# RWKV-7 recurrence on one core: chunk systems inverted as two 16x16 diagonal blocks with the corner on TensorE; key path and masks on GpSimd, gram copies on ScalarE

## The chip, the cores and the metric

One core of a Trainium2 chip runs the whole program. The metric is the device time of one execution in microseconds; the comparison is made on medians of several executions.

## What is computed

The program is a chain of layers (attention, a retrieval feed-forward layer, two more mixers with their feed-forward layers). The change touches only the last mixer, an RWKV-7 time mixing over 256 tokens, 16 heads of 64:

```python
def rwkv7_step(state, inp):
    r_t, w_t, k_t, v_t, a_t, b_t = inp
    sa = jnp.einsum('bhvk,bhk->bhv', state, a_t)
    state = (state * w_t[:, :, None, :] + sa[..., None] * b_t[:, :, None, :]
             + v_t[..., None] * k_t[:, :, None, :])
    return state, jnp.einsum('bhvk,bhk->bhv', state, r_t)
...
    a = jax.nn.sigmoid((a0 + (xa @ a1) @ a2).astype(f32))
...
    kk = heads(k * k_k.astype(f32))
    kk = kk / jnp.maximum(jnp.sqrt(jnp.sum(kk * kk, axis=-1, keepdims=True)), 1e-12)
    k = k * (1.0 + (a - 1.0) * k_a.astype(f32))
...
    seqs = (tm(r_h), tm(w_h), tm(k_h), tm(v_h), tm(-kk), tm(kk * a_h))
    _, y = lax.scan(rwkv7_step, jnp.zeros((B, H, N, N), f32), seqs)
```

The kernel does not scan token by token. It works in chunks of 32 tokens (`C`), 8 chunks (`CT`) in 2 tiles (`NT`) of 128 tokens. Within a chunk the tokens depend on each other through a strictly triangular 32x32 matrix for each head, so a unit triangular system has to be inverted for each of the 32 pairs of tile and head (`NS`) in each of the 4 chunks of a tile; across chunks a 64x64 state for each head is carried.

## The kernel before, in words

`project_mixes` (L2958) makes the projections R, K, V in twelve weight blocks: ScalarE casts a block (`make_high`), VectorE makes its low half (`make_low`, L3080), TensorE multiplies, ScalarE empties the bank (L3064). In its last two blocks VectorE also makes `raw` = K times the row k_k, its sums and its normalisation (L3124 to L3133). GpSimd does nothing in it. Each such function is one `nc.Block`; the engines meet at its end, and the next function starts when the last of them has finished.

`wkv` (L3145) is the recurrence. Each engine has a queue of its own written out by hand, and the queues meet in semaphores. In order of time:

1. Low-rank products on TensorE, their biases added by VectorE (L3571) in the order L tile 0, A tile 0, L tile 1, A tile 1; sigmoids on ScalarE (L3476); sums of the decays on TensorE (L3281); exponentials on ScalarE (L3469, L3487) into `up`, `down`, `before`.
2. VectorE makes the scaled operands: `key_factor` (L3582), `rate_key` (L3588), `scale_r` (L3592), `scale_keys` (L3598, L3600) for each tile, later `key` (L3585) and `tt(Kd, K, down)` (L3611, L3616). Each is one pass over 128x1024 floats.
3. TensorE turns each scaled operand (`flip`, L3304), in eight jobs: r, a, kk of tile 0, the same of tile 1, then k of both. ScalarE and VectorE place the turned halves (`place`, L3218 to L3223), and `grams` (L3312) multiplies them: 128 small matmuls for each of four calls.
4. VectorE masks the grams out of PSUM (`mask`, L3558): those of a into `GA`, those of k into `GK`.
5. VectorE inverts all the systems at once: it transposes 32x32 blocks (L3620), runs 31 steps of a product (L3625) and a sum (L3627), and transposes back (L3636). The masks of `GK` (after steps 4 and 10) and the products `K * rest` (after step 14, L3634) stand inside this loop.
6. Meanwhile TensorE makes the remaining decays (L3335), the decays at the chunk ends (L3340), the products within a chunk (L3349, which need `GK`), and the key-value products (L3358). ScalarE empties them (L3511, L3515).
7. With the inverses and all of `KV` in place, TensorE applies the inverses (`w2` L3366, `w1` L3375), and seven steps carry the state from chunk to chunk (`write` L3387, read L3423, `grow` L3647). Normalisation and gate follow; `mix_out_to_end` (L3753) is the next block.

GpSimd clears two tiles at the start (L3746, L3748) and one later (L3750). SyncE loads three rows at the start of `wkv`. `slot(i)` is a buffer of the weight ring, 128x2048 floats; slots 4 and 5 hold the inversion.

Of the kernel before, what the change touches and what calls it, by code (L numbers as in the profile page):

```python
# [19 lines left out]
ALU = mybir.AluOpType  # L20
# [122 lines left out]
class Kit:  # L143
# [17 lines left out]
    def dve(self, ins):  # L161

        self.nc.vector.wait_ge(self.step["dve"].sem, self.step["dve"].up(ins))

# [2793 lines left out]
def project_mixes(kit, dram, R, K, V, A, KK, L, G, rs):  # L2958
# [19 lines left out]
    kk_row, biases = place(6)[:, 0:D], place(9)  # L2978
# [3 lines left out]
    with kit.sb("mix_high", [P, 2, KD, SEQ], F32R) as x_hi, kit.sb("mix_low", [P, 2, KD, SEQ], F32R) as x_lo, \  # L2982
# [7 lines left out]
        def _(sp):  # L2990
# [6 lines left out]
            kk_in.up(sp.dma_start(kk_row, bcast(dram["rw_kk_2"], D)), 16)  # L2997
            sp.wait_ge(split.sem, p0 + 10)
# [78 lines left out]
        def _(dve):  # L3077
# [26 lines left out]
            for b in range(1, nb):  # L3104
# [15 lines left out]
                if b == nb - 2:  # L3120
                    dve.wait_ge(kk_in.sem, 16)
# [23 lines left out]
def wkv(kit, dram, R, K, V, A, KK, L, G, wide_in, rows, chunks, Kd, turned1, twa, tgb, st, bonus, PC):  # L3145
# [29 lines left out]
    XT, terms = (slot(4)[:, i * C * C:(i + 1) * C * C].rearrange("p (j t) -> p j t", j=C) for i in range(2))  # L3175
    sy = slot(5)[:, 0:C * C].rearrange("p (j t) -> p j t", j=C)
    inv = slot(5)[:, C * C:2 * C * C].rearrange("p (u t) -> p u t", t=C)
# [12 lines left out]
    grams_a, grams_k, masked_a, masked_k = (kit.count(n) for n in ("grams_a", "grams_k", "masked_a", "masked_k"))  # L3190
    cleared, solved = kit.count("inverse_cleared"), kit.count("solved")
# [7 lines left out]
    with kit.sb("arT", [P, NT, 2 * KD, 5, C]) as arT, \  # L3199
            kit.sb("gram_a", [P, NS, 2 * C]) as GA, kit.sb("state", [P, KD, HD]) as S, \  # L3200
            kit.sb("state_part", [P, KD, HD]) as part, nc.Block() as block:
        GK = wide_in[:].rearrange("p t n -> p (t n)").rearrange("p (u j) -> p u j", j=2 * C)
# [37 lines left out]
        def _(sp):  # L3240
            for i, row in enumerate((dram["rw_ka_2"], dram["rw_rk_2"].rearrange("e h d -> e (h d)"))):
                rows_in.up(sp.dma_start(rows[:, i], bcast(row, D)), 16)
            rows_in.up(sp.dma_start(chunks[:], dram["chunks"]), 16)

            for T in range(NT):
                sp.wait_ge(within_out.sem, 4 * (T + 1))
                sp.wait_ge(masked_k.sem, 2 * NT)
# [16 lines left out]
        def _(pe):  # L3264
# [42 lines left out]
            def grams(T, keys, j, bank, columns_of, done):  # L3307
                for half in range(2):
                    wait_placed(pe, j, half)
                for hh in range(RH):  # L3310
# [3 lines left out]
                    if hh // 2 == KD - 1:  # L3314
                        done.up(mm)
# [3 lines left out]
            grams(0, BT, 2, 0, first_a, grams_a)  # L3319
# [3 lines left out]
            grams(1, BT, 5, 2, first_a, grams_a)  # L3323
            flip(6)
            grams(0, KT, 6, 6, block_of, grams_k)
            flip(7)
            pe.wait_ge(masked_a.sem, 2)
            grams(1, KT, 7, 0, block_of, grams_k)
# [79 lines left out]
            for n, T, c in steps[1:]:  # L3408
# [27 lines left out]
                if n in (CH, CH + 1):  # L3436
                    share(0, n - CH, range(CH))
# [549 lines left out]
```

## Time and profile before

| what | before |
|---|---|
| three runs | 2704.85, 2705.49, 2709.05 us; median 2705.49 |
| span of the profiled execution | 2706.4 us |
| busy in the span | TensorE 2380.3, VectorE 1862.4, ScalarE 1218.7, GpSimd 622.8 us |
| `wkv` in the span | 2349.55 to about 2485.5 us |
| GpSimd in `wkv` | three memsets |

The span is what the profiler recorded of one execution, from the first to the last instruction. Starts are microseconds from the start of the span. A row of the timeline has the start, the time taken, the engine, the line, the operation, what is written and read, the shapes, the number of instructions merged, and in brackets how long the engine was idle before it and what ended that ("issue" is a wait for nothing that the profile shows). PE is TensorE, DVE VectorE, ACT ScalarE, POOL GpSimd. Two further facts of the page are used below: queue 8 moved the instructions, 85 packets and 1.39 MB, some 16 KB each; TensorE had 12882 matmuls, each with a weight load.

### The profile page before, as it was taken

To read this page: it belongs to the slowest core of one execution; us is meant where nothing else is said; L and a number is where in the kernel's file an instruction comes from. 1 tells how busy PE (TensorE), PEld (TensorE's weight loads), DVE (VectorE), ACT (ScalarE), POOL (GpSimd) and SP (SyncE) were. 2 spreads that over 40 slices of the span, in tenths; PEclk is the share of its full clock that TensorE was granted. 3 is DMA by queue.
4 is the path that set the end of the run, shared out by engine and by line. 5 is a ranking of instruction groups with operands and counts; after the bars stand their busy time and mean duration, and the time that the engine had idled before them with its cause. 6 is when DMAs were issued, how large, how long until landed. Compare 5 with 4: busy or idle time off the path is not lost. (4 is left out here: it accounts for less than half of the span.)

```text
span 2706.4 us, 35151 instructions
## 1 busy us (share of the span) xinstructions
PE 2380.3 (88%) x12882; PEld 1586.5 (59%) x12882; DVE 1862.4 (69%) x3462; ACT 1218.7 (45%) x2588; POOL 622.8 (23%) x529
## 2 busy tenths in 40 slices
PE   6988788888888988888778799999999998977999
PEld 4774334333334444343333268898888887866887
DVE  4767866677667867867765666676667666797665
ACT  3433434444444544444434454457445444534543
POOL 0003444554444434455544400000000000000000
PEclk9988999999999999999999999999999998977999
DMA  9789999999999999999999945542555554212553
GB/s 386 257 329 423 403 427 427 424 427 424 424 411 418 376 426 411 427 427 427 427 424 426 427 160 186 186 156 98 183 186 181 188 188 165 91 50 111 179 187 116
DMA packets 121706, 811.27 MB, mean 300 GB/s; under 512 B 15713, under 2 KB 18825, under 8 KB 26584
## 3 DMA queue, kind: packets, MB, share of 16 engines
q0 software_dynamic: 74160, 540.05, 47.7%
q1 hardware_dynamic: 47400, 269.32, 27.5%
q8 instruction: 85, 1.39, 0.2%
q14 instruction: 61, 0.50, 0.0%
HBM read 807.12 MB, written 1.15 MB: 299 GB/s over the span
## 5 line engine op out<-in xcount | busy, mean ns | idle before, releaser
L1402 PE MATMUL bank<-rows,diag 128*128 128x512 f32 (+1 forms) x2060 | 995.9, 620 | 212.6 <-ACT diag L1559 212.1
L1797 DVE CUSTOM_DVE_ANT_0 rows<-rows,h 128x1024 f32<-128x1024 f32 (+1 forms) x512 | 620.3, 1224 | 359.7 <-DMA rows<-in_peer_rows,idx 353.3
L1402 PEld LDWEIGHTS bank<-rows,diag 128*128 128x128 f32 (+1 forms) x2060 | 371.8, 194 | 739.7 <-ACT diag L1559 421.1
L1281 POOL DMA_INDIRECT rows<-in_peer_rows,idx x512 | 609.0, 1189 | 741.5 <-PE bank L1402 679.3
L1550 ACT ACTIVATE picks<-picks 128x1 f32<-128x1 f32 (+1 forms) x512 | 103.3, 202 | 637.9 <-DVE picks L1797 617.5
L2142 PE MATMUL bank<-hT_pair,halves 128*128 128x512 f32 x864 | 307.2, 399 | 0.4 <-DVE hT_pair L2020 0.4
L2143 PE MATMUL bank<-hT_pair,halves 128*128 128x256 f32 x864 | 242.2, 280 | 0.0
L1559 ACT ACTIVATE diag<-const_table,picks 128x128 f32<-128x128 f32 (+1 forms) x512 | 205.5, 401 | 48.0 <-ACT picks L1554 1.1
L2076 DVE TENSOR_TENSOR halves<-weight_ring,halves 128x2048 fp32r<-128x2048 f32 x74 | 169.3, 2289 | 74.3 <-ACT halves L2071 74.1
L2142 PEld LDWEIGHTS bank<-hT_pair,halves 128*128 128x128 f32 x864 | 162.3, 188 | 40.9 <-DVE hT_pair L2020 0.9
L1314 PE MATMUL bank<-halves_b,halves_a 128*128 128x256 f32 x912 | 172.0, 331 | 0.0
L2071 ACT CAST halves<-weight_ring 128x2048 fp32r<-128x2048 f32 x74 | 141.3, 1911 | 50.3 <-PE bank L2151 27.0
L2143 PEld LDWEIGHTS bank<-hT_pair,halves 128*128 128x128 f32 x864 | 163.1, 189 | 0.8
L1554 ACT ACTIVATE picks<-picks 128x1 f32<-128x1 f32 (+1 forms) x512 | 150.8, 294 | 18.9 <-ACT picks L1550 0.4
L1314 PEld LDWEIGHTS bank<-halves_b,halves_a 128*128 128x128 f32 x912 | 125.0, 191 | 55.7 <-issue 55.7
L2076 DVE TENSOR_TENSOR halves_b<-weight_ring,halves_b 128x2048 fp32r<-128x2048 f32 x36 | 82.5, 2292 | 63.7 <-ACT halves_b L2071 63.7
L2142 PE MATMUL bank<-hT_pair,halves_b 128*128 128x512 f32 x336 | 119.4, 398 | 1.5 <-DVE work L2252 1.5
L3746 POOL MEMSET weight_ring<- 128x1024 f32 x1 | 1.0, 952 | 499.7 <-POOLq L2985 499.7
L2151 PE MATMUL bank<-halves_a,hidden 128*128 128x512 f32 x320 | 103.7, 395 | 0.0
L2076 DVE TENSOR_TENSOR halves_a<-weight_ring,halves_a 128x2048 fp32r<-128x2048 f32 x36 | 82.4, 2289 | 25.1 <-ACT halves_a L2071 25.1
L2071 ACT CAST halves_a<-weight_ring 128x2048 fp32r<-128x2048 f32 x36 | 69.0, 1916 | 59.4 <-PE bank L2151 57.4
L2143 PE MATMUL bank<-hT_pair,halves_b 128*128 128x256 f32 x336 | 94.2, 280 | 0.0
(571 smaller groups left out, 3772.2 us busy)
## 6 DMA issues: line engine op xcount, KB each, us to landing
weight_ring<-in_ffn_w_gate SPq DMA_DIRECT2D x44, 1024.0 KB, 4.7
weight_ring<-in_ffn_w_up SPq DMA_DIRECT2D x44, 1024.0 KB, 4.8
weight_ring<-in_ffn_w_down SPq DMA_DIRECT2D x44, 1024.0 KB, 4.8
mod_ring<-in_mod_w SPq DMA_DIRECT2D x16, 1024.0 KB, 7.5
weight_ring<-in_peer_w_q SPq DMA_DIRECT2D x16, 1024.0 KB, 11.3
half_ring<-in_mod_w SPq DMA_DIRECT2D x24, 512.0 KB, 7.2
rows<-in_mod_w SPq DMA_DIRECT2D x12, 1024.0 KB, 8.1
weight_ring<-in_attn_w_in SPq DMA_DIRECT2D x12, 1024.0 KB, 4.7
```

The lines of the kernel that those rows point to most:

```text
L1281: nc.gpsimd.indirect_dma_start(ring[:, s], None, dram["peer_rows"], bass.IndirectOffsetOnAxis(ap=idx[:, T, n:n + 1], axis=0)).then_inc(row ...
L1314: mm = nc.tensor.matmul(kit.bank[hh % 2][:, half * SEQ:(half + 1) * SEQ], w[:, k, half * P:(half + 1) * P], t[:, :, k, :], start=(k == 0 a ...
L1402: mm = nc.tensor.matmul(bank[:, :], diag[0:n, j % DIAG_SLOTS], ring[0:n, j % ROW_SLOTS, D + half * 512:D + (half + 1) * 512], start=(j in ...
L1550: gelued.up(nc.scalar.activation(its_dot, its_dot, ACT.Gelu_apprx_tanh))
L1554: scaled.up(nc.scalar.activation(its_weight, its_dot, ACT.Copy, scale=its_gate))
L1559: weighed.up(nc.scalar.activation(diag[r, j % DIAG_SLOTS], eye[r], ACT.Copy, scale=its_weight))
L1797: dotted.up(nc.vector.tensor_tensor_reduce(out=ring[r, s, 0:D], in0=ring[r, s, 0:D], in1=its_h, scale=1.0, scalar=0.0, op0=ALU.mult, op1=A ...
L2071: self.kit.nc.scalar.copy(hi, w).then_inc(self.high_made.sem, 1)
L2076: self.kit.nc.vector.tensor_tensor(lo, w, hi.bitcast(F32), ALU.subtract).then_inc(self.split.sem, 1)
L2142: nc.tensor.matmul(bank[:, :], w_hi[:, k, cols], halves.pair[:, k, :], start=(k == 0), stop=False, skip_group_check=True)
L2143: mm = nc.tensor.matmul(bank[:, SEQ:2 * SEQ], w_lo[:, k, cols], halves.hi[:, k, :], start=False, stop=(k == KD - 1), skip_group_check=True)
L2151: mm = self.kit.nc.tensor.matmul(self.kit.bank[4 + 2 * T + half][:, :], hidden[:, f % 2, s, T * P:(T + 1) * P], w[:, s, half * 512:(half + ...
```

## The change

What it does:

- The inverse of a 32x32 unit triangular system is built of its two 16x16 diagonal blocks (15 steps over both at once, instead of 31 steps) and a corner block, which is a product of three matrices. Two groups of 128 small matmuls on TensorE make the corner, one group ahead of the chunk-end decays and one behind them; four matmuls with the identity bring the lower diagonal block into the bank to which the corner is added. ScalarE copies between them.
- The key path moves from VectorE to GpSimd: four passes in `project_mixes` (K times k_a, subtracted from K), six in `wkv` (products with a, sums, products with `down`).
- The grams are copied out of PSUM by ScalarE; GpSimd masks them in SBUF, the one of k before the products within a chunk, the second half of the one of a before the shares of tile 0.
- The biases are added in the order L tile 0, L tile 1, A tile 0, A tile 1. The row k_a is loaded in `project_mixes`.

```diff
@@ project_mixes
             kk_in.up(sp.dma_start(kk_row, bcast(dram["rw_kk_2"], D)), 16)
+            kk_in.up(sp.dma_start(ka_row, bcast(dram["rw_ka_2"], D)), 16)
...
+        @block.gpsimd
+        def _(pool):
+            pool.wait_ge(made.sem, NT)
+            for T in range(NT):
+                kit.pool(nc.gpsimd.tensor_tensor(rated_part[:, T], K[:, T], ka_row, ALU.mult))
+                kit.pool(nc.gpsimd.tensor_tensor(K[:, T], K[:, T], rated_part[:, T], ALU.subtract))
@@ wkv, TensorE
-            pe.wait_ge(masked_a.sem, 2)
-            grams(1, KT, 7, 0, block_of, grams_k)
-
-            pe.wait_ge(masked_a.sem, 4)
+            pe.wait_ge(grams_out.sem, 2)
+            grams(1, KT, 7, 0, block_of)
+
+            pe.wait_ge(grams_out.sem, 4)
             for q in range(4):
...
+            pe.wait_ge(grams_out.sem, 6)
+            pe.wait_ge(solved.sem, 1)
+            for u in range(NS):
+                for c in range(CH):
+                    mm = nc.tensor.matmul(kit.bank[6][chunk(c), u * HC:(u + 1) * HC], GA[chunk(c), u, 0:C], own_blocks[chunk(c), u, 0:HC],
+                                          start=True, stop=True, tile_position=(c * C, c * C))
+            corner.up(mm)
+            for c in range(CH):
+                nc.tensor.matmul(kit.bank[7][chunk(c), :], kit.ident[chunk(c), chunk(c)], own_blocks[chunk(c), :, HC:],
+                                 start=True, stop=True, tile_position=(c * C, c * C))
             pe.wait_ge(exped.sem, 11)
...
             summed.up(mm)
+            pe.wait_ge(placed.sem, len(on_act) + 1)
+            for u in range(NS):
+                for c in range(CH):
+                    mm = nc.tensor.matmul(kit.bank[7][c * C:c * C + HC, u * HC:(u + 1) * HC], corner_t[chunk(c), u, :],
+                                          own_blocks[chunk(c), u, HC:], start=False, stop=True, tile_position=(c * C, c * C),
+                                          skip_group_check=True)
+            corner.up(mm)
             pe.wait_ge(exped.sem, 15)
 
             for T in range(NT):
-                pe.wait_ge(masked_k.sem, 2 * T + 2)
+                pe.wait_ge(masked.sem, T + 1)
+                if T:
+                    pe.wait_ge(placed.sem, len(on_act) + 2)
...
+                if n == CH:
+                    pe.wait_ge(masked.sem, NT + 1)
@@ wkv, ScalarE
-            place_next(len(on_act) - 4)
+            place_next(5)
+            copy_grams(GA, 0, 0)
+            copy_grams(GA, 1, 2)
+            place_next(2)
+            copy_grams(GK, 0, 6)
+            place_next(2)
+            copy_grams(GK, 1, 0)
             for T in range(NT):
                 exps(rest, T, 2 + 2 * T, -1.0, 5 + 2 * T)
+            act.wait_ge(corner.sem, 1)
+            placed.up(nc.scalar.copy(corner_t, kit.bank[6][:, :].rearrange("p (u t) -> p u t", t=HC)))
             act.wait_ge(summed.sem, 9)
...
+            act.wait_ge(corner.sem, 2)
+            placed.up(nc.scalar.copy(inv[:, :, HC:], kit.bank[7][:, :].rearrange("p (u t) -> p u t", t=HC)))
@@ wkv, VectorE
             def rate_key(T):
+                dve.wait_ge(key_rated.sem, T + 1)
                 step(tt(A[:, T], A[:, T], KN[:, T], mul))
...
-            key_factor(0)
             rate_key(0)
...
-            key(0)
             place_half(3)
-            k_scaled.up(tt(Kd[:, 0], K[:, 0], down[:, 0], mul))
-            mask(GA, P + 2 * C, grams_a, masked_a, 0, 0)
-            key(1)
             place_half(4)
             place_half(5)
-            k_scaled.up(tt(Kd[:, 1], K[:, 1], down[:, 1], mul))
-            mask(GA, P + 2 * C, grams_a, masked_a, 1, 2)
-
-            dve.wait_ge(masked_a.sem, 2 * NT)
+
+            dve.wait_ge(k_scaled.sem, NT)
+            dve.wait_ge(grams_out.sem, 2 * NT)
             step(nc.vector.transpose(sy.rearrange("p j t -> p t j"), GA[:, :, 0:C].rearrange("p u t -> p t u")))
...
-            for i in range(C - 1):
-
-                n, later = C - 1 - i, XT[:, 0:i + 1, i + 1:]
...
+            for i in range(HC - 1):
+                n, later = HC - 1 - i, x_blocks[:, :, 0:i + 1, i + 1:]
+                final = x_blocks[:, :, 0:i + 1, i].unsqueeze(3).to_broadcast([P, 2, i + 1, n])
+                shares = s_blocks[:, :, i, i + 1:].unsqueeze(2).to_broadcast([P, 2, i + 1, n])
+                step(tt(terms[:, :, 0:i + 1, 0:n], final, shares, mul))
+                step(tt(later, later, terms[:, :, 0:i + 1, 0:n], add))
+
+            nc.vector.transpose(own_blocks[:, :, 0:HC].rearrange("p u t -> p t u"), XT[:, 0:HC, :])
+            solved.up(nc.vector.transpose(own_blocks[:, :, HC:].rearrange("p u t -> p t u"), XT[:, :, HC:].rearrange("p j t -> p t j")))
+            solved.up(nc.vector.transpose(inv[:, :, 0:HC].rearrange("p u t -> p t u"), XT[:, :, 0:HC].rearrange("p j t -> p t j")))
+            for T in range(NT):
+                dve.wait_ge(exped.sem, 12 + 2 * T)
+                k_state.up(tt(K[:, T], K[:, T], rest[:, T], mul))
+            dve.wait_ge(solved.sem, 2)
@@ wkv, GpSimd
+            gtt = nc.gpsimd.tensor_tensor
+            for T in range(NT):
+                pool.wait_ge(rated.sem, NT + T + 1)
+                key_rated.up(gtt(rated_part[:, T], rated_part[:, T], A[:, T], ALU.mult))
+            for T in range(NT):
+                pool.wait_ge(key_rated.sem, T + 1)
+                kit.pool(gtt(K[:, T], K[:, T], rated_part[:, T], ALU.add))
+                pool.wait_ge(exped.sem, 5 * T + 4)
+                k_scaled.up(gtt(Kd[:, T], K[:, T], down[:, T], ALU.mult))
...
+            pool.wait_ge(rows_in.sem, 32)
+            for T in range(NT):
+                pool.wait_ge(grams_out.sem, 2 * NT + 2 * T + 2)
+                masked.up(mask(GK[:, T * RH:(T + 1) * RH, :], P, 2 * C))
+            masked.up(mask(GA[:, :, C:], P + 3 * C, C))
             pool.wait_ge(within_out.sem, 4 * NT)
```

## Rows read from the trace of the kernel before

**Rows 1.** Chain that ended last, 2349 to 2490 us: start, us, what.

```profile
2485.51 0.07 issue
...
2485.64 1.91 ACT halves L2071
```

**Rows 2.** Timeline, VectorE in `wkv`: start, us, engine, line, operation.

```profile
2363.01 1.22 DVE L3582 SCALAR_TENSOR_TENSOR key_decayed<-A,key_rows 128x1024 f32<-128x1024 f32 x1
...
2386.53 2.13 DVE L3620 STREAM_TRANSPOSE weight_ring<-gram_a 128x1024 f32<-128x1024 f32 x1
2388.69 0.19 DVE L3625 TENSOR_TENSOR weight_ring<-weight_ring 128x31 f32<-128x31 f32 x1
...
2391.18 0.30 DVE L3627 TENSOR_TENSOR weight_ring<-weight_ring 128x135 f32<-128x135 f32 x1
...
2416.76 2.07 DVE L3636 STREAM_TRANSPOSE weight_ring<-weight_ring 128x1024 f32<-128x1024 f32 x1
...
2423.48 2.36 DVE L3655 TENSOR_TENSOR weight_ring<-weight_ring,key_rows 128x1024 f32<-128x1024 f32 x2
2425.87 0.69 DVE L3642 COPY weight_ring<-bank 128x512 f32<-128x512 f32 x1
...
2428.39 0.82 DVE L3647 TENSOR_TENSOR state<-weight_ring,bank 128x256 f32<-128x256 f32 x2
```

**Rows 3.** Timeline, TensorE in `wkv`.

```profile
2373.96 1.48 PE L3312 MATMUL bank<-arT,hT 64*32 64x64 f32 x128
...
2383.21 2.04 PE L3312 MATMUL bank<-arT,turned_keys 64*32 64x64 f32 x128 [0.88 <-DVE arT L3221]
...
2394.27 3.70 PE L3335 MATMUL bank<-L,chunk_table 128*128 128x512 f32 x8
2397.81 3.63 PE L3340 MATMUL bank<-const_table,L 128*128 128x4 f32 x32
2401.75 5.61 PE L3349 MATMUL bank<-V,KK 32*64 32x64 f32 x250 [0.31 <-ACT chunk_decay L3506]
...
2411.47 1.80 PE L3358 MATMUL bank<-V,K 32*64 32x64 f32 x127 [2.97 <-issue]
2415.32 0.80 PE L3358 MATMUL bank<-V,K 32*64 32x64 f32 x34 [2.05 <-issue]
2418.97 0.28 PE L3366 MATMUL bank<-weight_ring 32*32 32x64 f32 x1 [2.86 <-DVE weight_ring L3636]
...
2426.33 0.73 PE L3375 MATMUL bank<-weight_ring,removal 32*64 32x32 f32 x33 [0.96 <-issue]
```

**Rows 4.** Timeline, ScalarE in `wkv`.

```profile
2391.89 0.59 ACT L3223 COPY turned_keys<-bank 128x512 f32<-128x512 f32 x1 [0.27 <-PE bank L3304]
...
2416.16 2.05 ACT L3515 COPY weight_ring<-bank 128x512 f32<-128x512 f32 x4 [2.02 <-PE bank L3358]
```

**Rows 5.** Groups of GpSimd by line: count, busy us, mean ns of one, idle before.

```profile
L2585 POOL TENSOR_TENSOR weight_ring<-weight_ring,const_table 128x384 f32<-128x384 f32 x4 | 4.0, 1007 | 294.1 <-DVE weight_ring L2640 294.1
```

**Rows 6.** Timeline, GpSimd beside VectorE in the retrieval layer.

```profile
1229.85 1.22 DVE L1797 CUSTOM_DVE_ANT_0 rows<-rows,h 128x1024 f32<-128x1024 f32 x1
1229.98 1.91 POOL L1281 DMA_INDIRECT rows<-in_peer_rows,idx  x1 [3.06 <-PE bank L1402]
...
1234.45 0.94 POOL L1281 DMA_INDIRECT rows<-in_peer_rows,idx  x1 [0.55 <-PE bank L1402]
...
1234.54 0.41 DVE L1950 MATCH_REPLACE8 hT<-ranks,hT 128x256 f32<-128x256 f32 x1
```

**Rows 7.** Timeline, the end of `project_mixes`, VectorE and ScalarE.

```profile
2339.17 2.29 DVE L3080 TENSOR_TENSOR low<-weight_ring,high 128x2048 fp32r<-128x2048 f32 x1 [1.20 <-ACT high L3037]
...
2344.62 2.36 DVE L3133 TENSOR_TENSOR weight_ring<-weight_ring,key_norms 128x1024 f32<-128x1024 f32 x2
...
2348.70 0.59 ACT L3064 COPY V<-bank 128x512 f32<-128x512 f32 x1 [4.50 <-PE bank L3023]
```

**Rows 8.** Busy time in a stretch: length, engines, granted clock, DMA share.

```profile
2380.00:2390.00 10.00, 6.74 (x269) 5.76 (x270) 7.90 (x13) 1.17 (x2) 0.00 (x0) 0.60 0.01 3
```

More of the change, by code:

```diff
@@ L163, in dve, with pool @@
         self.nc.vector.wait_ge(self.step["dve"].sem, self.step["dve"].up(ins))
+    def pool(self, ins):
+        self.nc.gpsimd.wait_ge(self.step["pool"].sem, self.step["pool"].up(ins))
     def act(self, ins):
@@ L3174, in wkv @@
     KV = W.ring[:, SLOTS // 2 + 1:SLOTS // 2 + 3, :].rearrange("p s (c n) -> p (s c) n", c=4)
[L3175 removed]
+    HC = C // 2
+    XT = slot(4)[:, 0:C * C].rearrange("p (j t) -> p j t", j=C)
+    terms = slot(4)[:, C * C:C * C + C * HC].rearrange("p (b j t) -> p b j t", b=2, t=HC)
     sy = slot(5)[:, 0:C * C].rearrange("p (j t) -> p j t", j=C)
+    on_diagonal = lambda i: slot(i)[:, 0:C * C + C].rearrange("p (b n) -> p b n", b=2)[:, :, 0:HC * C].rearrange("p b (j t) -> p b j t", t=C)[:, :, :, 0:HC]
+    own_blocks = slot(5)[:, 0:C * C].rearrange("p (u t) -> p u t", t=C)
     inv = slot(5)[:, C * C:2 * C * C].rearrange("p (u t) -> p u t", t=C)
@@ L3189, in wkv @@
     turned, placed, placed_dve = kit.count("wkv_turned"), kit.count("wkv_placed"), kit.count("wkv_placed_dve")
-    grams_a, grams_k, masked_a, masked_k = (kit.count(n) for n in ("grams_a", "grams_k", "masked_a", "masked_k"))
-    cleared, solved = kit.count("inverse_cleared"), kit.count("solved")
+    grams_made, grams_out, masked, key_rated = (kit.count(n) for n in ("grams_made", "grams_copied", "grams_masked", "key_rated"))
+    rated_part = by_tile(slot(5))
+    cleared, solved = kit.count("inverse_cleared"), kit.count("diagonal_solved")
+    corner = kit.count("corner_product")
     parted = kit.count("state_decayed")
@@ L3240, in _ @@
         def _(sp):
-            for i, row in enumerate((dram["rw_ka_2"], dram["rw_rk_2"].rearrange("e h d -> e (h d)"))):
-                rows_in.up(sp.dma_start(rows[:, i], bcast(row, D)), 16)
+            rows_in.up(sp.dma_start(rows[:, 1], bcast(dram["rw_rk_2"].rearrange("e h d -> e (h d)"), D)), 16)
             rows_in.up(sp.dma_start(chunks[:], dram["chunks"]), 16)
@@ L3305, in flip, with grams @@
                     turned.up(mm)
-            def grams(T, keys, j, bank, columns_of, done):
+            def grams(T, keys, j, bank, columns_of):
                 for half in range(2):
@@ L3554, in _ @@
             tt, stt = nc.vector.tensor_tensor, nc.vector.scalar_tensor_tensor
-            def mask(G, at, grams, masked, T, b):
-                for i in range(2):
-                    dve.wait_ge(grams.sem, 2 * T + i + 1)
-                    masked.up(tt(G[:, T * RH + i:(T + 1) * RH:2, :], kit.bank[b + i][:, :].rearrange("p (a t) -> p a t", t=2 * C),
-                                 chunks[:, at:at + 2 * C].unsqueeze(1).to_broadcast([P, KD, 2 * C]), mul))
             def place_half(j):
@@ L3565, in _ @@
             dve.wait_ge(bias_in.sem, 32)
-            for T in range(NT):
-                for m, dst in enumerate((L, A)):
+            for m, dst in enumerate((L, A)):
+                for T in range(NT):
                     for i in range(2):
@@ L3577, in _ @@
                     biased.up(tt(quarter(before, 2 * T + i), kit.bank[4 + 2 * T + i][:, :], quarter(L, 2 * T + i), ALU.subtract))
-            dve.wait_ge(rows_in.sem, 48)
-            def key_factor(T):
-                dve.wait_ge(rated.sem, NT + T + 1)
-                step(stt(out=Kd[:, T], in0=A[:, T], scalar=-1.0, in1=rows[:, 0], op0=add, op1=mul))
-            def key(T):
-                step(stt(out=K[:, T], in0=Kd[:, T], scalar=1.0, in1=K[:, T], op0=add, op1=mul))
+            dve.wait_ge(rows_in.sem, 32)
             def rate_key(T):
+                dve.wait_ge(key_rated.sem, T + 1)
                 step(tt(A[:, T], A[:, T], KN[:, T], mul))
```

40 lines of the change are left out of this document (19 added, 21 removed).

## The prediction

> **What bounds the kernel now.** I read the chain of work that ended last first. It is of no use inside the recurrence: it enters at 2485.6 us, where the next block starts [rows 1]. The engines meet at the end of each block, so what counts is when the last of them leaves `wkv`, and that has to be read from the timelines. VectorE first [rows 2]: from the key factor at 2363.01 it is hardly idle until it has transposed the inverses back, 2416.76 + 2.07 = 2418.83. Its 62 instructions of inversion run from 2388.69 to 2416.76, 0.19 us each at the start and 0.30 us with 135 elements. Then TensorE [rows 3]: the first inverse is applied at 2418.97, and the bracket names VectorE. The reader is tempted to stop here and to count every microsecond taken from VectorE as won. But the same matmul also waits for `KV`, and ScalarE empties its last four banks at 2416.16 + 2.05 = 2418.21 [rows 4]. The two paths arrive 0.6 us apart. What VectorE wins is worth 0.6 us as long as the other path stays where it is, and the change puts work into that other path.
>
> I count to the start of `grow` (2428.39, rows 2); behind it nothing but order is changed, and a shift there goes through to the end.
>
> **VectorE's own path, GpSimd costing it nothing.** Out go two key factors, two `key`, two products with `down` and eight masks of 0.6 us. Up to the operands of tile 1 only the key factors were on the path (2 x 1.25 = 2.5 us), and ScalarE's exponentials give back little of it. VectorE then places the turned halves without other work between, so the second gram of a ends near 2381.7; ScalarE's two copies (0.59 each [rows 4]) end at 2383.1, where the transposition starts, against 2386.53 [rows 2]. It takes 2.13. The new loop has 30 instructions over 30 to 128 elements; from the 0.19 and 0.30 us of rows 2, and 0.04 between them, 0.29 each, 8.6 us. If the additional level of the access pattern costs, up to twice that; no row speaks for it. Two half transpositions of 1.05 follow: the diagonal blocks are out at 2383.2 + 2.2 + 8.6 + 2.1 = 2396.1. K and A times `rest` and the bonus products (9.4 us by four rows like 2423.48 [rows 2]) end before 2408, covered by TensorE.
>
> **TensorE's path.** The corner's first product waits for 2396.1; L3335 has ended some 4 us earlier than before, at 2394, so this wait is new and the chunk-end decays, the products within a chunk and the key-value products are all queued behind it. A group of 128 small matmuls takes 1.48 [rows 3] at best and 2.8 (5.61/2) at worst; with 16 columns I take 1.6. The identity products take 0.93 (3.70/4) if the four run together and 3.7 if not; they lie in four different corners of the array, I take 1.1. Chunk ends 3.63 as now; corner two 1.6. Both copies of ScalarE (0.59) lie beside the decays and beside tile 0. So the products within a chunk start at 2396.2 + 1.6 + 1.1 + 3.6 + 1.6 = 2404.1 against 2401.75, 2.4 us late. From there to the first inverse it is 17.2 us now, 0.6 of them waiting for VectorE: 2420.7, 1.7 late. Behind it VectorE now copies the bank late, at 2425.87, because of the bonus products [rows 2]; that gives back 0.5. Without any quarrel between GpSimd and VectorE the change is therefore worth **+1.2 us**: the loop alone loses 28.1 - 2.5 (masks) - 2.3 (K times `rest`) - 8.6 = 14.7 us, and nothing of it reaches the end.
>
> One cost is in no row by itself. TensorE stands still with "issue" for 2.97, 2.05 and 0.96 us [rows 3], between groups of about 128 small matmuls that start 3.85 us apart. The page's queue for instructions carried some 16 KB at a time, and 128 matmuls with their weight loads are 256 instructions; my reading is that code arrives no faster. The 260 new matmuls are two such portions: 0 if they are fetched in the wait and during the slow chunk ends, 2 x (3.85 - 1.9) = 3.9 if not. I take 0, since both pauses lie right there.
>
> **GpSimd.** It gets four passes in `project_mixes`, six in the key path and three masks, each over 1024 elements. The only such instruction now has 384 and takes 1.007 [rows 5]: 2.69 in proportion, 2.37 with 0.19 fixed as in the smallest of rows 2. I take 2.4. Does it run beside VectorE? In the retrieval layer GpSimd starts at 1229.98, while VectorE has been in an instruction with two SBUF inputs since 1229.85. It takes 1.91, which is the 1.09 left of that instruction and 0.8; at 1234.45, beside an instruction of VectorE with one large input, it takes 0.94 [rows 6]. So GpSimd gets no read while VectorE reads two operands. That the opposite holds too, VectorE standing while GpSimd reads, no row shows, because that GpSimd instruction reads only a column; I take it, as a shared way to SBUF that is given to one instruction at a time is the simplest cause.
>
> The Trainium skill, page "SBUF — State Buffer", section "Who interferes with whom", says it outright: "A DVE instruction with two SBUF inputs contends with a GpSimd instruction that reads SBUF", and whoever is first keeps the port for its whole instruction. The rows agree for one direction; this rule speaks against the change. The page "GPSIMD Engine Reference", section "Performance versus the Vector engine", has 4.50 us for 2048 elements, which would be an estimated 2.35 a pass.
>
> Taken so, the three places cost:
> - End of `project_mixes`: VectorE's last two-input passes are at 2339.17 (2.29) and 2344.62 (2 x 1.2), and the block ends with ScalarE at 2349.3 [rows 7]. GpSimd starts at 2338.1; its 9.6 us and VectorE's 4.7 alternate, with 0.4 of root between: the end is at 2352.4. **+3.1**. (Running freely it would end at 2347.8, hidden.)
> - Key path: VectorE has eight two-input passes from 2363.1. The first GpSimd pass lies beside its one-input work; each of the other five stands in front of one of them, 12.0 us, of which 1.5 were waits for exponentials and 1.6 waits for turned halves. **+8.9** at the transposition.
> - Masks: the three fall into the loop, where every instruction has two SBUF inputs: 3 x 2.4 = **+7.2**.
> Sum: 1.2 + 3.1 + 8.9 + 7.2 = 20.4. The profiled span is 2706.4, the median 2705.5; the difference is put on the median: **2725.9 us**.
>
> **Rivals.**
> 1. *No quarrel* (VectorE's passes keep their 1.22 us pitch, GpSimd is hidden): +1.2, 2706.7; with the bounds of the corner products and the code 2704.5 to 2711. For it: no row shows VectorE waiting for GpSimd. Against it: GpSimd waits for VectorE [rows 6], and what holds one can hold the other.
> 2. *One-sided*: GpSimd yields, VectorE never does. GpSimd then ends `project_mixes` at 2352 (+2.5), delays the rates of tile 1 and the transposition (2385.0 for 2383.2) and the masks: about +6, 2711.5.
> 3. *Faster*: no quarrel, and the code portions fall otherwise, so that the "issue" waits of 2.97, 2.05 and 0.96 [rows 3] go; TensorE, less idle between 2375 and 2392, may also keep the upper level of its clock: it was granted 0.60 of it in the mean of 2380 to 2390 [rows 8], where a gram took 2.04, after 1.48 before [rows 3], 1.1 for two. 1.2 - 6.0 - 1.1 = -5.9, 2699.6. It decides when the key-value products end before 2411. Against: more matmuls make this wait longer, not shorter.
> 4. *The halved loop isn't half*: each of its 30 instructions costs twice what rows 2 give for its size, because of its additional level: +8.6 on top of the first rival, 2715.3.
>
> **How the numbers follow.** Chances: the forecast 0.58 (its own range 2719 to 2733, by a pass of 2.37 to 2.69, a clock that falls in the longer pauses, and 0 to 3.9 for code), no quarrel 0.22, one-sided 0.10, faster 0.08, loop 0.02. The range 2705 to 2733 leaves out the faster case, the low third of "no quarrel" and a tail above. A measurement of this kernel can tell about 0.2% (5.4 us) from no change: faster takes its own 0.08; same takes "no quarrel" and half of "one-sided", 0.27; slower 0.65.
>
> **What will show it.** VectorE's `scale` passes after 2363 spaced 3.6 us rather than 1.25, each idle naming GpSimd or nothing; three gaps of some 2.4 us in the 30-step loop; the first instruction of `wkv` 3 us late. The loop without its gaps 8.6 us. The chunk ends behind the first corner, and the first inverse naming ScalarE's `KV` copy in its bracket, not VectorE. Wrong if VectorE and GpSimd overlap at full speed, or if the key-value products run without "issue" waits.

## The result, and the profile after

The changed kernel takes **2743.8 us** (median of 4 runs, 2742.84 to 2744.15) against 2707.27 (2704.85 to 2714.43): 1.0128 of the time before, 95% interval 1.0115 to 1.014. The forecast was 2725.9 with a range of 2705 to 2733: the sign was right, the loss nearly twice the forecast one, 36.5 us for 20.4.

The profiled execution has a span of 2742.4 us. From run to run the hundreds of microseconds ahead of the recurrence vary by several us whatever the kernel, so I count from one mark in all kernels: the start of VectorE's products of keys and the `kk` row near the end of `project_mixes` (L3124 before at 2335.62, L3130 after at 2333.46). From there to the end it is 370.8 us before and 408.9 after, **+38.2**. The stations between, in us from that mark, are read off the timelines:

```
                                  before   after   after-before   forecast
transposition of gram_a starts     50.91   59.84       +8.9         +8.7
first product of a chunk (V,KK)    66.13  100.30      +34.2        +21.6
first product with an inverse      83.35  119.03      +35.7        +20.9
grow starts                        92.77  129.97      +37.2        +20.4
end                               370.78  408.94      +38.2        +20.4
```

(The forecast's column: its times without a quarrel, and the 3.1, 8.9 and 7.2 us of GpSimd put where they lie.) The first station is met to 0.2 us. Nearly all that was missed lies between the transposition and `grow`.

Timelines of GpSimd (first fence) and VectorE (second) after, columns as in [rows 2], where a VectorE pass over 1024 elements with two inputs from SBUF took 1.22 us:

```profile
2335.89 2.42 POOL L3145 TENSOR_TENSOR weight_ring<-K,weight_ring 128x1024 f32<-128x1024 f32 x1 [487.02 <-DVE weight_ring L3130]
2338.38 4.33 POOL L3146 TENSOR_TENSOR K<-K,weight_ring 128x1024 f32<-128x1024 f32 x1
...
2370.96 3.22 POOL L3794 TENSOR_TENSOR key_decayed<-K,weight_ring 128x1024 f32<-128x1024 f32 x1
```

```profile
2343.61 5.96 DVE L3139 TENSOR_TENSOR weight_ring<-weight_ring,key_norms 128x1024 f32<-128x1024 f32 x2
...
2362.96 2.48 DVE L3626 TENSOR_TENSOR weight_ring<-bank,L 128x512 f32<-128x512 f32 x4
2365.37 3.31 DVE L3631 TENSOR_TENSOR A<-A,weight_ring 128x1024 f32<-128x1024 f32 x1
...
2378.47 3.38 DVE L3631 TENSOR_TENSOR A<-A,weight_ring 128x1024 f32<-128x1024 f32 x1
2381.88 1.22 DVE L3635 TENSOR_TENSOR R<-R,weight_ring 128x1024 f32<-128x1024 f32 x1
...
2393.30 2.15 DVE L3656 STREAM_TRANSPOSE weight_ring<-gram_a 128x1024 f32<-128x1024 f32 x1 [2.78 <-ACT gram_a L3545]
...
2397.29 2.30 DVE L3664 TENSOR_TENSOR weight_ring<-weight_ring 128x96 f32<-128x96 f32 x1
...
2401.20 2.33 DVE L3664 TENSOR_TENSOR weight_ring<-weight_ring 128x126 f32<-128x126 f32 x1
2403.57 2.30 DVE L3663 TENSOR_TENSOR weight_ring<-weight_ring 128x128 f32<-128x128 f32 x1
...
2459.03 0.69 DVE L3678 COPY weight_ring<-bank 128x512 f32<-128x512 f32 x1 [36.60 <-PE bank L3404]
...
2463.43 0.84 DVE L3683 TENSOR_TENSOR state<-weight_ring,bank 128x256 f32<-128x256 f32 x2 [0.46 <-PE bank L3425]
```

On GpSimd a pass takes 2.42 us alone and up to 4.33 when it has to wait for VectorE. On VectorE five passes in a row take 3.3 us, and the next one, when GpSimd has finished, 1.22 again. In the loop exactly three instructions of 96 to 128 elements take 2.3 us instead of under 0.3, one for each mask. The four passes at 2362.96, which read one input from PSUM, lie beside a GpSimd pass and take 2.48 for four halves, no more than without it. And then VectorE is idle for 36.60 us. Whatever the engines do to each other, that is where the result is made, on TensorE:

```profile
2399.71 3.70 PE L3354 MATMUL bank<-L,chunk_table 128*128 128x512 f32 x8
2412.34 1.90 PE L3359 MATMUL bank<-weight_ring,gram_a 32*32 32x16 f32 x127 [8.93 <-DVE weight_ring L3667]
2416.34 1.90 PE L3359 MATMUL bank<-weight_ring,gram_a 32*32 32x16 f32 x128 [2.10 <-issue]
2420.09 0.18 PE L3359 MATMUL bank<-weight_ring,gram_a 32*32 32x16 f32 x1 [1.85 <-issue]
2420.10 1.93 PE L3363 MATMUL bank<-weight_ring,const_table 32*32 32x512 f32 x8
2421.96 6.99 PE L3369 MATMUL bank<-const_table,L 128*128 128x4 f32 x32
2428.88 1.98 PE L3374 MATMUL bank<-weight_ring,gram_a 32*16 32x16 f32 x215
2433.30 0.53 PE L3374 MATMUL bank<-weight_ring,gram_a 32*16 32x16 f32 x41 [2.45 <-issue]
2433.76 2.62 PE L3387 MATMUL bank<-V,KK 32*64 32x64 f32 x87
```

A corner product is written as 128 calls, but the trace has 127 + 128 + 1 = **256** matmuls for it: every fp32 matmul is recorded twice (the grams of [rows 3], 64 calls, have 128). TensorE runs 127, stands for 2.10 us under "issue", runs 128, stands again. Then the chunk ends take 6.99 us where they took 3.63 [rows 3]. From 2412.2, when VectorE hands over the diagonals, to 2433.76 it is 21.6 us; the forecast had 8.0. Busy time in two stretches of 10 us (columns as in [rows 8]), and the queues' packets in 2410 to 2440:

```profile
2415.00:2425.00 10.00, 6.80 (x152) 5.04 (x151) 7.35 (x7) 0.59 (x1) 0.00 (x0) 0.50 0.01 3
2425.00:2435.00 10.00, 7.55 (x321) 7.40 (x324) 0.00 (x0) 0.81 (x2) 0.00 (x0) 0.50 0.01 3
```

```profile
GB/s 0 0 0 0 0 22 0 0 0 0 22 0 0 0 0 22 0 0 0 0 0 0 0 0 0 0 0 22 0 0 0 0 22 0 0 0 0 22 0 0
...
q8 instruction: 6, 0.10, 1.3%
```

The granted clock is 0.50, the 1.2 GHz level. And nothing moves in these 30 us but six packets of the instruction queue, 16 KB each, never less than five slices of 0.75 us apart. The first three in slices of 0.25 us, from 2412 to 2422, and behind it the same view of the wait, 2400 to 2413.5:

```profile
GB/s 0 0 0 0 0 0 0 66 0 0 0 0 0 0 0 0 0 0 0 0 0 0 66 0 0 0 0 0 0 0 0 0 0 0 0 0 0 0 66 0
...
DMA packets 0, 0.00 MB, mean 0 GB/s; under 512 B 0, under 2 KB 0, under 8 KB 0
```

The packets start in the slices at 2413.75, 2417.50 and 2421.50. Each starts 1.2 to 1.7 us after TensorE has begun a group (2412.34, 2416.34, 2420.09), and the next group begins 2.3 to 2.6 us after a packet's start (2416.34, 2420.09). During the 8.93 us in which TensorE waits for VectorE, none moves. The reading that fits these times is that the next portion is called for when TensorE has entered the one before it, and a stop of about 2 us follows wherever a portion is used up sooner than the next can come. Two suspects for the same 13.5 us, then: the clock, and the arrival of instructions. The experiments had to tell them apart, and both from GpSimd.

### The profile page after: what moved, and what is told of

It is laid out like the page before. It is cut to its first block and busy times, and to the rows that moved or that the text cites. A ratio compares the mean times of both kernels' runs of the same rounds, so it can differ in the third digit from the quotient of the medians.

```text
span 2742.4 us, 36172 instructions
## 1 busy us (share of the span) xinstructions
PE 2397.7 (87%) x13402; PEld 1600.5 (58%) x13402; DVE 1858.9 (68%) x3418; ACT 1224.8 (45%) x2598; POOL 665.9 (24%) x542
## 5 line engine op out<-in xcount | busy, mean ns | idle before, releaser
L3145 POOL TENSOR_TENSOR weight_ring<-K,weight_ring 128x1024 f32<-128x1024 f32 x2 | 4.8, 2410 | 487.1 <-DVE weight_ring L3130 487.0
```

## The experiments

The same stations for the twelve kernels, us from the mark in each one's profiled execution (before, e2, e5 and e12 have one transposition there, the others release TensorE after the second of three; e5 and e12 have no corner; "solved" is the end of the transpositions that release TensorE):

```
run                          transp.  solved  (V,KK)  inverse    grow     end   end-before
before                         50.91   83.21   66.13    83.35   92.77  370.78
after                          59.84   78.74  100.30   119.03  129.97  408.94     +38.2
e1 inversion only              51.34   66.57   87.55   106.68  116.17  396.17     +25.4
e2 GpSimd only                 59.70   95.67   73.54    95.82  105.23  385.26     +14.5
e3 half the corner             61.74   80.65   94.50   112.87  122.17  400.90     +30.1
e4 warm                        61.72   79.83   99.60   118.66  128.33  405.77     +35.0
e5 no corner                   51.33   66.66   67.72    84.42   94.05  371.57      +0.8
e6 masks late                  59.27   72.09   93.34   112.11  123.06  401.50     +30.7
e7 chunk ends first            59.84   78.83   91.25   110.22  121.99  399.01     +28.2
e8 key passes in wkv           55.65   74.64   95.66   113.97  124.09  401.32     +30.5
e9 all three moved             56.04   68.91   82.10   100.27  112.04  388.65     +17.9
e10 wide corner                59.97   79.08  100.06   119.06  129.18  405.94     +35.2
e11 e1, chunk ends first       51.33   66.54   79.10    97.83  107.32  385.51     +14.7
e12 e5, half the key-value     51.33   66.68   65.03    77.48   87.37  365.04      -5.7
```

`grow` to the end is 276.6 to 280.0 in all of them, so end-before, read from one execution each, carries a scatter of up to 3 us. The medians have a shift of their own: the kernel before had 2707.27 us beside the changed kernel, 2708.42 beside e1 to e4, 2710.41 beside e5 to e8 and 2708.7 beside e9 to e12. Where a median is compared below with that of after, these 1.1 to 3.1 us come on top (e6 lies 5.6 us under after as the medians stand, 8.7 with each less its own before). The ratios and the counts from the mark are free of it.

**The two halves of the change, each alone.** In the kernel before, the split inversion and the corner as in the diff, the rest left on VectorE:

```diff
-            for i in range(C - 1): ...
+            for i in range(HC - 1): ...        # masks of K still at i = 4 and 10
+            # TensorE: corner 1, identity product, chunk ends, corner 2, as in the change
```

> The kernel before with the split inversion and the corner on TensorE (placed as in the kernel after), but the key path, the masks and the gram copies left on VectorE. Theory A (the corner's cost is the number of instructions that TensorE must be fed, the port's cost is a separate sum): the diagonals are out at about 2404.5 instead of 2414.3 in the time of before, since no GpSimd pass blocks VectorE, and the corner takes the same 21.5 us from the diagonals to the first product inside the chunks; so about 10 us of the 36 are gone and it is 24 to 28 us over before. Theory B (the corner is as cheap as I forecast, 8 us, and GpSimd is to blame for nearly all): 5 to 12 us over before.

Measured: 2731.65 us, 1.0082 of before (1.0065 to 1.0098), and +25.4 from the mark. The diagonals are out at 66.57, 12 us sooner than in the kernel after, GpSimd does nothing, and from them to the products of a chunk it is still 21.0 us. Theory A; GpSimd isn't needed for the larger part.

The other half: the kernel after with before's loop of 31 steps and no corner.

```diff
-            for i in range(HC - 1): ...
+            for i in range(C - 1): ...         # k_state at i = 14, no masks
-            # TensorE: corner 1, identity product, corner 2
```

> The kernel after with before's whole inversion of 31 steps put back and no corner: key path and masks on GpSimd, grams copied by ScalarE. Theory A: the transposition is 9 us later (2.4 of it from the end of the token mixes), the masks' passes block the loop for 6 us where VectorE's own masks took 5, so 9 to 12 us over before; with the first run's 24 to 28 it adds up to the 36 measured. Theory B: 25 us or more over before.

Measured: 2725.9 us, 1.0054 (1.0036 to 1.0073); +14.5 from the mark, of which +8.8 stand at the transposition and +12.5 at the end of the inversion; the last 2 us come behind `grow` and are within the scatter. A little above the 9 to 12 expected, and 25.4 + 14.5 = 39.9 for the whole change's 38.2. The halves add up, because in both the same chain of transposition, inversion and TensorE is lengthened.

**Instructions or execution?** Every second system's corner left out (the corners of the odd systems are not computed):

```diff
-            for u in range(NS):
+            for u in range(0, NS, 2):
```

> The kernel after with every second system's two corner products left out (64 calls each instead of 128; the corners of the odd systems are then not computed). Theory A (TensorE waits for its instructions, about 3.9 us for every 128 recorded matmuls): 128 recorded matmuls less in each group, 7 to 8 us under after. Rival (only execution counts, 1.90 us for 127): 3.8 us under after.

Measured: 2736.98 us, 6.8 under after; from the diagonals to (V,KK) 13.9 us instead of 21.6, -7.7. TensorE in this kernel:

```profile
2419.30 1.90 PE L3359 MATMUL bank<-weight_ring,gram_a 32*32 32x16 f32 x127 [8.96 <-DVE weight_ring L3667]
2423.03 0.18 PE L3359 MATMUL bank<-weight_ring,gram_a 32*32 32x16 f32 x1 [1.83 <-issue]
...
2431.81 1.26 PE L3374 MATMUL bank<-weight_ring,gram_a 32*16 32x16 f32 x128
```

128 recorded matmuls less save 4.0 us in the first product and 3.7 in the second, where 128 of them are busy for 1.90 and 1.26. That is the instruction theory's number. Next the clock: five matmuls of 128x512 into bank 7 fill TensorE's wait.

```diff
             pe.wait_ge(grams_out.sem, 6)
+            for n in range(5):
+                nc.tensor.matmul(kit.bank[7][:, :], chunks[:, 0:P], quarter(L, n % 4), start=True, stop=True)
             pe.wait_ge(solved.sem, 1)
```

> The kernel after with five matmuls of 128x512 into a free bank while TensorE waits for the diagonals, so that its clock is up when the corner starts. Theory A: the corner's groups stay 3.9 us apart, since they wait for instructions; only the chunk ends (6.99 us, 3.63 in the kernel before) fall back, 2 to 4 us under after. Rival (the granted clock of 0.50 is the whole cause): everything between the diagonals and the first product inside the chunks halves, 8 to 11 us under after.

Measured: 2743.43 us, no difference that can be told from after. From the diagonals to (V,KK) 19.8 us, 1.8 less. TensorE, and the busy time and clock between the filler's last matmuls and the corner and inside the corner:

```profile
2412.92 4.46 PE L3357 MATMUL bank<-L,chunk_table 128*128 128x512 f32 x10
2421.80 3.50 PE L3361 MATMUL bank<-weight_ring,gram_a 32*32 32x16 f32 x246 [4.43 <-DVE weight_ring L3669]
2426.90 0.34 PE L3361 MATMUL bank<-weight_ring,gram_a 32*32 32x16 f32 x9 [1.60 <-issue]
...
2428.96 6.99 PE L3371 MATMUL bank<-const_table,L 128*128 128x4 f32 x32
...
2415.00:2421.00 6.00, 2.38 (x6) 0.76 (x4) 5.45 (x18) 0.00 (x0) 0.28 (x1) 1.00 0.00 0
2422.00:2425.00 3.00, 3.00 (x240) 3.00 (x235) 3.00 (x4) 0.00 (x0) 0.00 (x0) 0.50 0.02 5
```

The run doesn't do what it was built for. Behind the filler TensorE still waits 4.43 us, and the granted clock, 1.00 up to 2421, is 0.50 from the start of the corner on, so the corner and the chunk ends (6.99 again) both run at the lower level here too. The 1.8 us don't come from the clock. The filler shifts where a portion of instructions ends: 246 matmuls went without a stop, instead of 127. This run says nothing of the clock; e6, below, does, by accident.

Next the work in a call. Twice the columns in each call of the first corner (the corners come out wrong), as many instructions:

```diff
-  bank[6][chunk(c), u * HC:(u + 1) * HC], GA[chunk(c), u, 0:C], own_blocks[chunk(c), u, 0:HC]
+  bank[6][chunk(c), u // 2 * C:(u // 2 + 1) * C], GA[chunk(c), u, 0:C], own_blocks[chunk(c), u, :]
```

> The kernel after with 32 columns instead of 16 in each call of the first corner product (pairs of systems then write the same columns, so the corners come out wrong); as many instructions as before. Theory A (instructions): the first corner product still takes 7.8 us with its groups 4.0 us apart; no change in the whole, within 1 us. Rival (TensorE's work in columns): its busy time doubles and shows on the path, 2 to 4 us over after.

Measured: 2745.09 us (after 2743.8), and from diagonals to (V,KK) 21.0 for 21.6. The busy time, which the rival had doubled, doesn't even move:

```profile
2413.18 1.92 PE L3359 MATMUL bank<-weight_ring,gram_a 32*32 32x32 f32 x127 [9.15 <-DVE weight_ring L3667]
2416.63 1.93 PE L3359 MATMUL bank<-weight_ring,gram_a 32*32 32x32 f32 x128 [1.53 <-issue]
2420.66 0.21 PE L3359 MATMUL bank<-weight_ring,gram_a 32*32 32x32 f32 x1 [2.10 <-issue]
```

**What a free corner would bring.** e1 with both corner products, the identity product and their copies left out (the corners of the inverses stay zero):

```diff
-            # TensorE: corner 1, identity product, corner 2; ScalarE: their copies
```

> The first experiment with both corner products, the identity product and their copies left out (the corners of the inverses stay zero), so the halved loop is had for nothing. Theory A (TensorE's stream of small matmuls is the bound behind the gram masks): the inverse is out 16 us sooner than before, but TensorE comes to its first product with an inverse at most 2 us sooner, since it is fed the products inside the chunks and the key-value products until then; 0 to 2.5 us under before. So no corner on TensorE, however cheap, could win more. Rival (the inversion is the bound, and a free corner would bring its 15 us home): 10 us or more under before.

Measured: 2709.9 us, 0.9994 (0.9983 to 1.0004), +0.8 from the mark. The inverse is out 16.6 us sooner than before, and nothing comes of it: from the first product of a chunk to the first with an inverse it is 16.7 us for 17.2, 0.5 less where the forecast had 0.6, and from the chunk ends to `grow` 30.3 for 30.6. TensorE in this kernel, with ScalarE's copy of `KV` in the bracket where [rows 3] have VectorE:

```profile
2405.75 5.02 PE L3355 MATMUL bank<-V,KK 32*64 32x64 f32 x223 [0.31 <-ACT chunk_decay L3512]
...
2415.38 1.99 PE L3364 MATMUL bank<-V,K 32*64 32x64 f32 x127 [2.45 <-issue]
2419.50 0.80 PE L3364 MATMUL bank<-V,K 32*64 32x64 f32 x34 [2.13 <-issue]
2422.45 0.31 PE L3372 MATMUL bank<-weight_ring 32*32 32x64 f32 x1 [2.15 <-ACT weight_ring L3521]
```

So the split inversion couldn't have won anything here, even at no cost at all. The counterpart takes away instructions instead: the key-value products of every second head left out as well.

```diff
-                for hh in range(RH):           # key-value products
+                for hh in range(0, RH, 2):
```

> The fifth experiment (no corner at all) with the key-value products of every second head left out too, 64 calls less. Theory A (behind the gram masks TensorE is fed at about 3.9 us for 128 recorded matmuls, and that is what bounds the kernel): the first product with an inverse and all that follows it come 3.5 to 4.5 us sooner than in the fifth experiment. Rival (something else holds TensorE there, ScalarE's copies or a clock): less than 1.5 us sooner.

Measured: 2705.42 us, 0.9987 of before (0.9971 to 1.0002), against e5's 2709.9 and 0.9994; each less its own before it is 2.8 us under e5, and by the medians alone the two can hardly be told apart. From the mark it is 6.5 us sooner than e5, but 2.7 of it stand already at the start of the chunk ends (63.8 and 61.1 us from the mark), up to where the kernels don't differ and e5's grams ran at the lower clock. From the chunk ends to `grow` it is 26.3 us instead of 30.3, **-4.0** for 64 calls: theory A's number. A microsecond taken from VectorE is worth nothing here; 128 recorded matmuls taken from TensorE are worth 4.

**The places.** GpSimd's masks held until the diagonals are out:

```diff
             pool.wait_ge(rows_in.sem, 32)
+            pool.wait_ge(solved.sem, 1)
```

> The kernel after with GpSimd's masks held until the diagonals are out. Port theory: no instruction of the loop takes 2.3 us, the loop takes 8.6 us instead of 14.8, the diagonals are out and everything behind them is 6 us earlier, 6 us under after. Rival (the three instructions of 2.3 us are late for another reason): no change.

Measured: 2738.22 us, 5.6 under after; from the mark -7.4. The loop has no instruction over 0.3 us left, and from the transposition to the diagonals it is 12.8 us instead of 18.9. That VectorE and GpSimd hold each other up shows once more from the other side: the products with `rest` (2.3 us for two elsewhere), now beside the masks, take 6.00:

```profile
2411.85 6.00 DVE L3671 TENSOR_TENSOR K<-K,weight_ring 128x1024 f32<-128x1024 f32 x2
```

This kernel also separates the clock, since TensorE waited only 2.62 us and began the corner at its upper level (granted 1.00 from 2411.0 to 2412.4, 0.50 from 2413 to 2419):

```profile
2411.13 1.23 PE L3359 MATMUL bank<-weight_ring,gram_a 32*32 32x16 f32 x127 [2.62 <-DVE weight_ring L3667]
2415.13 1.90 PE L3359 MATMUL bank<-weight_ring,gram_a 32*32 32x16 f32 x128 [2.76 <-issue]
```

127 matmuls in 1.23 us rather than 1.90, and the next group begins 4.00 us after them, as in the kernel after (2412.34 to 2416.34); in e1, e3, e8 and e10, at the lower level, it is 3.45 to 3.73. The packet between the two groups starts 1.7 us after the first and 2.3 us ahead of the second, again as in the kernel after. What execution saves, "issue" takes back. For this group the clock is worth nothing; the corner's other groups ran at the lower level in every kernel, so for them it is not shown.

The chunk ends (16 calls, recorded as 32 matmuls) ahead of the corner, in TensorE's idle time:

```diff
+            # the 32 matmuls of the chunk ends
             pe.wait_ge(grams_out.sem, 6)
             pe.wait_ge(solved.sem, 1)
```

> The kernel after with the chunk ends' 32 matmuls ahead of the corner, in TensorE's idle time before the diagonals are out. If they only took time of their own on the path: 7.0 us under after. Theory A (their 6.99 us also hid the arrival of the second corner's instructions): from the diagonals to the products inside the chunks 15 to 16 us instead of 21.4, 5 to 6 us under after.

Measured: 2738.04 us, 5.8 under after; from the mark -9.9, from the diagonals to (V,KK) 12.4 us instead of 21.6. That is more than either number expected. The 6.99 are gone (they take 3.63 in the idle time, at the upper clock), the first corner is shorter by 2.9 and the second longer by only 1.0:

```profile
2409.20 3.63 PE L3360 MATMUL bank<-const_table,L 128*128 128x4 f32 x32
2418.08 3.18 PE L3365 MATMUL bank<-weight_ring,gram_a 32*32 32x16 f32 x223 [5.25 <-DVE weight_ring L3667]
2422.47 0.62 PE L3365 MATMUL bank<-weight_ring,gram_a 32*32 32x16 f32 x33 [1.22 <-issue]
```

My number for this run had left out where the portions end. 32 matmuls moved ahead leave 127 - 32 = 95 of the portion in use, and the next 128 were there as well: 223 without a stop. In the kernel after, TensorE waited 8.93 us one matmul into a fresh portion, and the next one had not been fetched (no packet between 2400 and 2413.5, above).

GpSimd's first four key passes at the start of the recurrence:

```diff
-            # project_mixes, GpSimd: K * ka, K - K * ka, for both tiles
+            # wkv, GpSimd, ahead of everything that waits for A: the same
```

> The kernel after with GpSimd's first four key passes at the start of the recurrence instead of the end of the token mixes, where VectorE reads PSUM or nothing while they run. Port theory: the mixes end as before (the make-low pass is back at 2.29 us and the two key-norm passes at 1.2 us each), 4 us under after. Rival (GpSimd's passes delay VectorE wherever they stand): 0 to 2 us under after.

Measured: 2740.26 us, 3.5 under after. The mixes end as before (first passes of `wkv` at 19.76 us from the mark, after 23.89), and the transposition is 4.2 us sooner. The port's theory gave 4 there. From the mark to the end it is 7.6; of the additional 3.4, 1.7 lie behind `grow`, within the scatter there; the other 1.7 accrue at TensorE's stops, and no run assigns them.

All three at once:

> The kernel after with all three changes of place at once: the masks held until the diagonals are out, the chunk ends ahead of the corner, GpSimd's first key passes at the start of the recurrence. If the three are separate costs, as the single runs showed them (about 7, 9 and 4 to 7 us between the key products and the end), the sum is 20 to 23 us under after, 13 to 17 over before: what is left is the corner's own instructions (about 12 us) and the key path's port conflict (about 4 us). Rival (they overlap): less than 16 us under after.

Measured: 2726.77 us, 17.0 under after, 1.0062 of before (1.0037 to 1.0087); from the mark -20.3 and 17.9 over before. The expectation had 20 to 23 under and 13 to 17 over, so it is met at its edge. Where each move acts, it gives nearly what it gave alone: 3.8 us at the transposition (4.2 in e8), 6.0 from there to the diagonals (6.1 in e6), 8.4 from the diagonals to (V,KK) (9.1 in e7). Over the whole, the three alone give 24.9 us from the mark, all at once 20.3; the costs of place are mostly separate, and 4.6 us, some of it scatter, are not accounted for. And e1 with the chunk ends first:

> The first experiment (inversion split, all key work on VectorE) with the chunk ends ahead of the corner. Theory A: 8 to 10 us under the first experiment, as in the kernel after; about 15 to 18 us over before, since the corner's instructions still stand in TensorE's way. Rival (with VectorE free, the early diagonals now pay): 5 us over before or less.

Measured: 2722.77 us, 1.0049 of before (1.0035 to 1.0063); -10.7 to e1 and +14.7 to before from the mark (8 to 10 and 15 to 18 were expected). It is the best form of the split inversion with nothing left out that I ran, without GpSimd, with the diagonals out 16.7 us before the old inverse, and it loses. No kernel that does the whole computation came under the one before.

## Why the prediction was wrong in size

- **Transposition at +8.7** (mixes +3.1, key path, less what VectorE saves): measured +8.9, of it +4.1 at the first pass of `wkv`. The mixes cost 1.0 more than said. Right.
- **A GpSimd pass 2.4 us, and VectorE stands for it**: 2.36 to 2.49 alone. The rows of GpSimd beside VectorE [rows 6] showed only that GpSimd waits; that VectorE waits too was taken on trust and is now in the rows: 3.3 us for 1.22, five times in a row. The Trainium skill's "SBUF — State Buffer", section "Who interferes with whom", is borne out by the trace in both directions (GpSimd 4.33 us for 2.40, VectorE 3.3 for 1.22), and by e6 and e8, which move the passes and get the time back. The rivals "no quarrel" and "one-sided" fall. One detail was wrong: I looked for gaps of idle time; the wait is inside the instruction's own duration.
- **Masks +7.2**: three instructions of 2.3 us in place of 0.3 each, 6.1, and e6 gives it back. I had added GpSimd's pass to an undisturbed instruction.
- **The loop 8.6 us without them**: in e6, without the masks, 8.7 us, and 12.8 from the transposition to the diagonals against 12.9 forecast. Right; the rival "the halved loop isn't half" falls.
- **Corner products 1.6 us each, on the argument of 128 matmuls a group**: this is the step that failed. The grams in [rows 3] are 64 calls and x128; I took x128 for 128 calls (item 3 of the kernel before in words says so too), and the corner's 128 calls are x256. All that followed was built on half the work: "260 new matmuls are two portions", when 520 new ones are four.
- **Portions of code at 0, since the wait and the chunk ends lie there**: the mechanism was named from [rows 3] and was the right one, the price wasn't. A wait of 8.93 us bought nothing (127 matmuls and a stop), since no packet comes while TensorE waits, and the range's end of 3.9 was again for half the number. Measured, first corner with identity 9.6 us for 2.7, second 4.9 for 1.6.
- **Chunk ends 3.63 "as now"**: 6.99, from a clock at 0.50. I let the clock in for "a pause that falls longer" in the range but kept the duration of a row at the upper level, behind a wait that the change itself makes longer. 9.6 + 7.0 + 4.9 = 21.5 for 8.0: **+13.5 us**, three quarters of the miss.
- **16.6 us on to the first inverse, then less to `grow`**: 18.7 and 10.9, +4.2 in all, at the lower clock (0.53 in 2445 to 2455) and with stops of 1.88 to 2.39 us. That these are the cause is argued, not shown: in the kernels with a corner the first stretch is 18.2 to 19.1, the second 9.3 to 11.8, and no run isolates either. The last 1.0 lies behind `grow` and is scatter.
- **"What VectorE wins is worth 0.6 us"**: right, and the most useful line of the forecast. In e5 the stretch in front of the first inverse is 0.5 us shorter than before, and the whole is the same to within 1 us.

Together: 0.2 + 13.5 - 1.1 + 4.2 + 1.0 = 17.8, and 20.4 + 17.8 = 38.2.

What stays open: how far TensorE must be inside a portion before the next is fetched. Ahead of the corner 1 recorded matmul was not enough (after, e1, e3, e6), and 11 (e4) and 33 (e7, e11) were; nothing between was run. Open too are the 4.2 us between (V,KK) and `grow`, the 1.7 us of e8 and the 4.6 by which e9 stays behind its parts.

## What to carry to other kernels

Before an inversion or a loop is shortened on one engine, ask who else must arrive at the same point; the cheapest answer is a run in which the work is left out altogether, like e5. On TensorE count small matmuls as the trace records them, calls times two in fp32, and price a stream of them at its pace of instructions, here about 4 us for every 128 recorded, not at its busy time. A wait ahead of such a stream doesn't make it cheaper, unless TensorE has already gone some way into the portion; a few matmuls put ahead of the wait did that in e4 and e7. GpSimd passes over SBUF were free here only beside VectorE work that reads PSUM or one input, and a step that is to be slow at a cold clock belongs ahead of the wait, not behind it.

## What the runs showed of the hardware that I had not expected

- TensorE's instructions come in packets of 16 KB while the kernel runs, one at a time; with small matmuls, where TensorE stops between groups of 128, they begin 3.3 to 4.6 us apart, 4.00 both with 1.23 us of work in a group and with 1.90. The Trainium skill, "Trainium Architecture — The Big Picture", section "The software stack", gives 64 bytes to an instruction; an estimate from that is 256 instructions in 16 KB, which agrees with 128 matmuls and their 128 weight loads; it also says that the streams are brought to the engines when the program is loaded, and there the measurement differs (six packets in the 30 us above).
- Waiting doesn't always fill the buffer: 127 matmuls were at hand after a wait of 8.93 us, 223 after 5.25 (and after 1.88 in e11) and 246 after 4.43. Where the portion stood counted, not how long TensorE waited.
- A matmul of 32x32 by 16 columns and one by 32 columns cost the same, 1.90 and 1.92 us for 127 at the lower clock.
- VectorE's last transposition in e6 lies beside GpSimd's first mask and takes 1.12 us, for 1.09 in e1 without GpSimd: one input from SBUF isn't held up.
